# Gated linear attention over 256 tokens: from a chain of sixteen-token chunks to recursive halving in one block

## The chip, the cores and the metric

One NeuronCore of a Trainium2 chip runs the whole kernel. The metric is device time in microseconds, the median of three runs. The profile is one further execution, recorded by the hardware profiler; the time that it took is given beside the span of its trace.

## The reference

One layer of a hybrid decoder over 280 tokens: 256 prompt tokens, 8 decode tokens (one for each of 8 sequences) and 16 meta tokens ahead of the prompt. The layer is a half-step SwiGLU FFN, a mixing stage, and a second half-step FFN, with a norm ahead of each and one at the end. Everything is fp32, D_MODEL is 2048, D_FF is 5632. The mixing stage projects the tokens once and runs two branches side by side: sliding-window attention with 16 heads, and gated linear attention (GLA) with 4 heads of key size 128 and value size 256. Gates then merge the two. The part that the change is about is the GLA branch over the prompt:

```
b   = cumsum(log decay)                        # per token, head and key channel
att[t, s] = sum_d q[t,d] * k[s,d] * exp(b[t,d] - b[s,d])      for s <= t
o   = att @ v + (q * exp(b)) @ S
S   = S * exp(b_last) + (k * exp(b_last - b)).T @ v
```

The difference b[t] - b[s] is never positive for s <= t, but exp(-b[s]) alone can overflow, so the decay can't simply be split into a factor of t and a factor of s over long distances. The meta tokens come first and leave a state S that the prompt starts from; the state after the last prompt token is an output. A decode token updates and reads a state of its own.

## The kernel before

**Slabs.** Each weight matrix is read as slabs of 128 output columns: 16 tiles of 128x128 (11 for the FFN's second matrix). A slab goes through four engines, always with two buffers. SyncE's queue loads it to `raw` (`load_slab`, 1 MB). ScalarE rounds it to `w_hi` (`split_hi`, L623). VectorE writes `w_lo = raw - w_hi` (`split_lo`, L957). TensorE does 48 matmuls of 264 or 280 token columns: hi weights by hi and lo activations (L1352, L1353), then lo weights by hi activations (L1358). Then VectorE takes the sum out of `bank[0]` or `bank[1]` and scales it. `slab_done` counts slabs, `bank_free` their evacuations. A slab waits for the bank of the slab two before it; the split of a slab waits until the slab two before it has been used. There are 404 slabs, in a fixed order: FFN1, `SWA_IN` (12 slabs), `GLA_IN` (16), `GATE_A` (16), `GLA_R` (8), `GATE_B` (12), the merge, `W_OUT`, FFN2. Every engine's program is written out by hand in that order. All that is not a slab is put between two slabs, on each engine by its own code, with semaphores between them.

**The other branch.** During `GLA_IN` the sliding-window attention of the prompt runs between the slabs (`scores`, `turn_scores`, `weigh_values`). During the first eight slabs of `GATE_A` (the loop over `e`) its decode part follows: at e = 3 the scores of eight tokens (L1504, L1505), at e = 7 their values (L1524, L1525), each 32 pairs of fp32 matmuls with 8 columns. Its windows are loaded by ScalarE's DMA queue (`load_windows`), in eleven transfers, eight of them of one row.

**GLA before.** At e = 2 TensorE multiplies the decay's low-rank factor up (L1495); ScalarE and VectorE make log decays of it and `tensor_tensor_scan` sums them into `bc`, in blocks of 32 tokens. After e = 7 the prompt goes through a loop of eight steps (`pair_of_slabs`), each with 32 tokens and two slabs of `GATE_A` or `GLA_R`. In a step, for each of two chunks of 16 tokens, VectorE writes all pairs' differences, 128x1024 (L334, L336); ScalarE takes their exp (L261); VectorE multiplies by keys and queries (L341, L343); and TensorE sums over the channels with 16 fp32 matmuls against a band of ones (`attend`, L386). Between the two chunks a matmul at the boundary does (`attend_across`, L395). Then 12 transposes (`turn`), four products of keys and values for the state (`keys_by_values`, L407), and 16 for the outputs (`outputs`, L423, L425) that lie inside the next step's slab, one after each second k. The step's state update (`new_state`, L359) is on VectorE; GpSimd scales the queries (`queries`, L567) and copies the values (`values`, L563). The last step's outputs and state follow after the loop. The decode part needs the new values split into hi and lo (`v_split`): eight transposes (L1559), ScalarE's zero fill (L868) and two copies (L874), VectorE's two subtractions (L1225). TensorE waits for these (`nv_lo`) ahead of L1585, the first matmul of `GATE_B`.

Of the kernel before, what the change touches and what calls it, by code (L numbers as in the profile page):

```python
# [40 lines left out]
CK = 16  # L41
CP = 2 * CK
NCP = NP_ // CP
# [22 lines left out]
def build_layer(nc, t):  # L66
    ctx = ExitStack()
    with ctx:
# [21 lines left out]
        gadT = sb("gadT", [P, TA])  # L90
# [8 lines left out]
        band = sb("band", [P, 2 * CP - 1])  # L99
# [6 lines left out]
        causal = sb("causal", [CP, 2, GH, CK])  # L106
        a_up = sb("a_up", [P, GH * DK])
# [4 lines left out]
        vbuf = sb("vbuf", [P, 8, CP])  # L112
        eend = sb("eend", [P, GH])


        R = sb("scratch", [P, 6816])
# [21 lines left out]
        sc = at(3060, 2, 4, 272)  # L138
        pT = at(5236, 3, 512)
        v_tok = at(1408, 2, 256)  # L140

        kT_win = at(3232, NS, 2, WIN + 1)
# [7 lines left out]
        v_meta_s = at(3232, NS, 256, parts=NM)  # L150

        oT = at(0, 8, TR)
        spl, mnz = at(5300, GH, TA), at(2112, GH, TA)
        bc = mnz
        scan_keep = at(512, TA)
        S = at(3232, GH, DV)
        Pd = at(4256, CK, GH, CK)
        k_tok = at(5280, 512, parts=CP)
        gv_tok = at(5792, 1024, parts=CP)
        a_smp = a_up[:, TR + GH * CP:TR + GH * CP + GH * NS].rearrange("p (h n) -> p h n", h=GH)  # L160
        kd = a_up[:, TR:TR + GH * CP].rearrange("p (h c) -> p h c", h=GH)

        def halves(tiles):

            return tiles.rearrange("p (x h) c -> p x h c", x=2)


        mid, edl = hT[:, 0:8, M0:TA], hT[:, 8:16, M0:TA]
        qd, attT = proj[:, 16:24, M0:TA], proj[0:CP, 24:32, M0:TA]

# [7 lines left out]
        r_act, r_sg = a_up[:, 0:TR], gadT[:, 0:TR]  # L178
        siga = proj[:, 16:32, 0:TR]
        merged = proj[:, 0:16, 0:TR]  # L180
# [23 lines left out]
        kwin_loaded, kmeta_loaded, vwin_loaded, vmeta_loaded, knew_done, qpad_done = (  # L204
            sem(n) for n in ("kwin_loaded", "kmeta_loaded", "vwin_loaded", "vmeta_loaded", "knew_done", "qpad_done"))
        swa_pe, swa_act, swa_dve, win_out = (sem(n) for n in ("swa_pe", "swa_act", "swa_dve", "win_out"))
        scan_loaded, bias_loaded = sem("scan_loaded"), sem("bias_loaded")
        z_done, prep_act, prep_dve = sem("z_done"), sem("prep_act"), sem("prep_dve")
        (g_eb, g_dl, g_edl, g_kd, g_diff, g_exp, g_pk, g_P, g_att, g_attT, g_kt, g_vt, g_ktok, g_vtok,
         g_vbuf, g_qd, g_o, g_oT, g_kv, g_S) = (sem(n) for n in (  # L210
            "g_eb", "g_dl", "g_edl", "g_kd", "g_diff", "g_exp", "g_pk", "g_P", "g_att", "g_attT", "g_kt",
            "g_vt", "g_ktok", "g_vtok", "g_vbuf", "g_qd", "g_o", "g_oT", "g_kv", "g_S"))
# [9 lines left out]
        g_mid, g_emid, g_kq = sem("g_mid"), sem("g_emid"), sem("g_kq")  # L222
# [15 lines left out]
        def columns(v, width, start=0):  # L238
            return slice(v * width + start, (v + 1) * width) if isinstance(v, int) else bass.ds(v * width + start, width - start)

        def pair_cols(u):
            return slice(M0, TA) if isinstance(u, int) and u == 0 else columns(u - 1, CP)

        def by_half(a):
            return a.rearrange("p h (x c) -> p x h c", x=2)

        def later(u, n=1):
            return not isinstance(u, int) or u > n

        def key_decay(act, u):  # L250
            act.wait_ge(g_dl, u + 1)
            e = edl if later(u, 0) else edl[:, 0:GH]
            act.activation(e, e, ACT.Exp, scale=1.0 / TAU).then_inc(g_edl, 1)

        def mid_decay(act, u):
            act.wait_ge(g_mid, 2 * u)
            act.activation(mid, mid, ACT.Exp, scale=1.0 / TAU).then_inc(g_emid, 1)

        def token_decay(act, c):
            act.wait_ge(g_diff, 2 * c + 2)  # L260
            act.activation(Pd, Pd, ACT.Exp, scale=1.0 / TAU).then_inc(g_exp, 1)  # L261

        def start_decay(act, u):

            act.wait_ge(g_S, 4 * u)
            if later(u):
                act.wait_ge(g_o, u - 1)
            act.activation(eend[:].unsqueeze(2), bc[:, :, columns(u - 1, CP, CP - 1)], ACT.Exp, scale=1.0 / TAU)
            act.activation(halves(qd), by_half(bc[:, :, pair_cols(u)]), ACT.Exp, scale=1.0 / TAU).then_inc(g_eb, 1)

        def to_tokens(act, u):

            n = CP if later(u, 0) else CK
            act.wait_ge(g_vt, u + 1)
            if later(u, 0):
                act.wait_ge(g_kv, u)
            if later(u):
                act.wait_ge(g_o, u - 1)
            act.activation(gv_tok[0:n, 0:512], bank[4][0:n, :], ACT.Copy).then_inc(g_vtok, 1)
            act.activation(gv_tok[0:n, 512:], bank[5][0:n, :], ACT.Copy).then_inc(g_vtok, 1)  # L280
            act.wait_ge(g_kt, u + 1)
            act.activation(k_tok[0:n, :], bank[3][0:n, :], ACT.Copy).then_inc(g_ktok, 1)
# [671 lines left out]
        def _(dve):  # L954
# [141 lines left out]
            for u in range(8):  # L1096
# [4 lines left out]
                if u:  # L1101
                    out_lo(u - 1)
# [622 lines left out]
```

## Time and profile before

| | us |
|---|---|
| median of 3 runs (2499.45 to 2504.62) | 2500.59 |
| profiled execution | 2502.67 |
| its span | 2500.8 |
| TensorE matmuls busy | 2454.7 (98%) |
| TensorE weight loads busy | 2385.5 (95%) |
| VectorE busy | 1369.2 (55%) |
| ScalarE busy | 985.6 (39%) |
| GpSimd busy | 168.4 (7%) |

A fp32 matmul leaves two records in the trace, an fp32r matmul or a transpose one. Matmuls are pipelined, so the duration of one says little; the distance from one start to the next says what it costs. The granted clock is TensorE's, as a share of 2.4 GHz. The stage that the change touches begins at 1071 us in the trace (slab e = 1 of `GATE_A`) and ends at 1391 us (the first matmul of `GATE_B`).

### The profile page before, as it was taken

Reading aid. Unit: us, or ns where it says so; the run is one execution under the profiler, and the core shown is the slowest. Engines: PE = TensorE matmul, PEld = TensorE weight load, DVE = VectorE, ACT = ScalarE, POOL = GpSimd, SP = SyncE. Lnnn points to the kernel's source line nnn. Section 1 sums busy time; section 2 is a strip of 40 time slices with the busy share of each in tenths; the row PEclk is TensorE's granted clock in tenths of the full one; section 3 lists DMA queues with packets and bytes.
Section 4 is the critical chain, followed back from the end, with each engine's and each line's share of the span. In section 5 each row is a group of like instructions: output and inputs, shape, how many; then the busy total and the mean of one; then the engine's idle time right before and its main releaser. Section 6 shows DMA issues by size and latency. Waiting matters only on the chain.

```text
span 2500.8 us, 47207 instructions
## 1 busy us (share of the span) xinstructions
PE 2454.7 (98%) x19106; PEld 2385.5 (95%) x19106; DVE 1369.2 (55%) x1567; ACT 985.6 (39%) x1036; POOL 168.4 (7%) x188
## 2 busy tenths in 40 slices
PE   7999999999999999999999999999999999999997
PEld 6999999999999998898888989999999999999997
DVE  6555554554556545544556465555555555555554
ACT  4333333333333344454545543434333333333332
POOL 2000000000003200000000130021000000000015
PEclk9999999999999999997889999999999999999998
DMA  5445445444544453351112554455555545545544
GB/s 187 173 156 184 168 159 178 170 167 166 186 168 155 167 175 119 118 188 72 67 67 70 191 186 152 169 185 183 176 169 192 181 162 194 184 161 192 184 165 138
DMA packets 67740, 401.72 MB, mean 161 GB/s; under 512 B 8703, under 2 KB 12439, under 8 KB 32199
## 3 DMA queue, kind: packets, MB, share of 16 engines
q1 hardware_dynamic: 62960, 386.86, 44.4%
q0 software_dynamic: 3264, 11.79, 1.3%
q10 hardware_dynamic: 1447, 2.10, 0.3%
q8 instruction: 51, 0.84, 0.1%
q14 instruction: 18, 0.15, 0.0%
HBM read 391.43 MB, written 9.27 MB: 160 GB/s over the span
## 4 chain that ended last, share of the span: by engine, by line
PE 92%; DVE 3%; issue 2%; ACT 1%; POOL 1%; DMA 0%; DVEq 0%; SPq 0%; ACTq 0%; POOLq 0%
PE bank L1352 29%; PE bank L1358 29%; PE bank L1353 28%; PE bank L386 1%; PE bank L407 1%; DVE w_lo L957 1%; PE bank L425 1%; ACT w_hi L623 1%; DVE x_lo L962 1%; PE bank L1466 0%; PE bank L423 0%; PE bank L370 0%; POOL scratch L601 0%; PE bank L1574 0%; PE bank L1464 0%
## 5 line engine op out<-in xcount | busy, mean ns | idle before, releaser
L623 ACT ACTIVATE w_hi<-raw 128x2048 fp32r<-128x2048 f32 (+1 forms) x404 | 705.4, 1746 | 1239.7 <-PE bank L1358 1196.3
L957 DVE TENSOR_TENSOR w_lo<-raw,w_hi 128x2048 fp32r<-128x2048 f32 (+1 forms) x404 | 845.2, 2092 | 469.8 <-ACT w_hi L623 469.6
L1352 PE MATMUL bank<-x_hi,w_hi 128*128 128x264 f32 (+1 forms) x3456 | 906.6, 295 | 16.4 <-DVE x_lo L962 11.5
L1353 PE MATMUL bank<-x_lo,w_hi 128*128 128x264 f32 (+1 forms) x3456 | 888.4, 290 | 0.0
L1352 PEld LDWEIGHTS bank<-x_hi,w_hi 128*128 128x128 f32 x3456 | 658.0, 190 | 40.4 <-issue 19.4
L1353 PEld LDWEIGHTS bank<-x_lo,w_hi 128*128 128x128 f32 x3456 | 658.4, 191 | 0.0
L1352 PE MATMUL bank<-y_hi,w_hi 128*128 128x264 f32 (+1 forms) x2368 | 598.2, 288 | 6.1 <-DVE y_lo L1255 5.6
L1353 PE MATMUL bank<-y_lo,w_hi 128*128 128x264 f32 (+1 forms) x2368 | 596.7, 287 | 0.0
L1358 PE MATMUL bank<-x_hi,w_lo 128*128 128x264 f32 (+1 forms) x3456 | 496.1, 293 | 0.0
L1358 PEld LDWEIGHTS bank<-x_hi,w_lo 128*128 128x128 f32 x3456 | 459.3, 191 | 4.1 <-issue 2.3
L1352 PEld LDWEIGHTS bank<-y_hi,w_hi 128*128 128x128 f32 x2368 | 447.2, 189 | 7.5 <-DVE y_lo L1255 6.9
L1353 PEld LDWEIGHTS bank<-y_lo,w_hi 128*128 128x128 f32 x2368 | 447.9, 189 | 0.0
L1358 PE MATMUL bank<-y_hi,w_lo 128*128 128x264 f32 (+1 forms) x2368 | 322.6, 286 | 0.0
L1358 PEld LDWEIGHTS bank<-y_hi,w_lo 128*128 128x128 f32 x2368 | 303.2, 189 | 0.0
L1011 DVE SCALAR_TENSOR_TENSOR hT<-bank,hT 128x280 f32 (+3 forms) x128 | 56.4, 441 | 116.3 <-PE bank L1358 115.9
L986 DVE TENSOR_TENSOR scratch<-bank,rstd 128x280 f32<-128x280 f32 (+1 forms) x88 | 38.8, 441 | 131.2 <-PE bank L1358 131.2
L503 POOL MEMSET scratch<- 128x280 f32 x4 | 1.3, 334 | 1576.8 <-DVE scratch L986 1457.1
L980 DVE TENSOR_TENSOR scratch<-bank,rstd 128x280 f32<-128x280 f32 (+1 forms) x88 | 38.8, 441 | 119.3 <-PE bank L1358 119.3
L509 POOL TENSOR_TENSOR scratch<-scratch 128x264 f32<-128x264 f32 (+1 forms) x56 | 81.4, 1453 | 4.9
L507 POOL TENSOR_TENSOR scratch<-hT 128x264 f32 (+2 forms) x56 | 37.9, 676 | 125.5 <-DVE hT L1323 68.3
L1048 DVE SCALAR_TENSOR_TENSOR proj<-bank,rstd 128x280 f32<-128x280 f32 (+1 forms) x28 | 12.4, 442 | 58.9 <-PE bank L1358 58.8
L386 PEld LDWEIGHTS bank<-scratch,band 128*32 128x32 f32 x512 | 37.5, 132 | 4.1 <-issue 1.7
(244 smaller groups left out, 1203.4 us busy)
## 6 DMA issues: line engine op xcount, KB each, us to landing
raw<-in_w_in SPq DMA_DIRECT2D x176, 1024.0 KB, 4.8
raw<-in_w_out SPq DMA_DIRECT2D x128, 704.0 KB, 4.0
raw<-in_w_proj SPq DMA_DIRECT2D x52, 1024.0 KB, 4.8
raw<-in_w_merge SPq DMA_DIRECT2D x32, 1024.0 KB, 4.8
raw<-in_w_o SPq DMA_DIRECT2D x16, 1024.0 KB, 4.8
scratch<-in_state_in POOLq DMA_DIRECT2D x8, 512.0 KB, 4.3
out_state_s<-scratch POOLq DMA_DIRECT2D x8, 512.0 KB, 5.3
hT<-in_xT SPq DMA_DIRECT2D x4, 560.0 KB, 7.3
```

The source lines that it names most:

```text
L386: last = pe.matmul(cols, band[:, CP - 1 - m:2 * CP - 1 - m], Pd[:, s], start=(s == 0), stop=(half == 0 and s == CK - 1))
L407: last = pe.matmul(bank[6 + h // 2][:, (h % 2) * DV:(h % 2 + 1) * DV], k_tok[0:n, h * DK:(h + 1) * DK], gv_tok[0:n, h * DV:(h + 1) * DV], ...
L507: pool.tensor_tensor(sq[:, 0:T], h, h, ALU.mult).then_inc(sq_done, 1)
L509: pool.tensor_tensor(acc[:, 0:T], acc[:, 0:T], sq[:, 0:T], ALU.add).then_inc(acc_done, tiles)
L623: act.activation(w_hi[:, b, 0:kt * P], raw[:, b, 0:kt * P], ACT.Copy).then_inc(hi_split, 1)
L957: dve.tensor_tensor(w_lo[:, b, 0:kt * P], raw[:, b, 0:kt * P], w_hi[:, b, 0:kt * P].bitcast(F32), ALU.subtract).then_inc(lo_split, 1)
L980: dve.tensor_tensor(a_n[:, 0:T], bank[0][:, 0:T], rstd[:, 0:T], ALU.mult).then_inc(bank_free, 1)
L986: dve.tensor_tensor(b_n[:, 0:T], bank[1][:, 0:T], rstd[:, 0:T], ALU.mult).then_inc(bank_free, 1)
L1011: dve.scalar_tensor_tensor(hT[:, m, 0:T], bank[b][:, 0:T], 0.5, hT[:, m, 0:T], ALU.mult, ALU.add).then_inc(bank_free, 1)
L1352: pe.matmul(out, w, x[0][:, k, 0:T], start=(k == ks[0]), stop=False)
L1353: pe.matmul(out, w, x[1][:, k, 0:T], start=False, stop=False)
L1358: last = pe.matmul(out, w_lo[:, b, k * P:(k + 1) * P], x[0][:, k, 0:T], start=False, stop=(k == ks[-1]))
```

## The change

The chunks and their loop go. The prompt is taken as two tiles of 128 tokens, and `att` is built by levels: level B (1, 2, 4, ... 64) holds the pairs s, t that lie in the two halves of one block of 2B tokens. For such a pair the decay is exp(b_mid - b_s) times exp(b_t - b_mid), with b_mid at the end of the first half, and both factors are at most 1. So a level is: VectorE takes the differences (`diffs`, two operations of 128x512), ScalarE exp of 128x1024 (`decays`), VectorE the products with keys and queries (`products`, two of 128x512), TensorE eight fp32 matmuls 128x128 by 128 columns (`level`: 4 heads, 2 tiles), VectorE puts the pairs of the level into `att` by a mask (`place`, two `copy_predicated` of 128x512, PSUM source, uint8 mask). The diagonal is a level of its own (`D_`), level 64 has 64 columns, level 128 only four matmuls; ScalarE places these two. There are no passes by GpSimd in the levels; it makes the six masks during FFN1.

The levels are spread over 24 slabs, one or so behind each. The meta state is made at e = 8 and 9, the values turned at e = 10 and 11, the end-decayed keys turned at e = 14, the final state at e = 15 (eight matmuls of 256 columns), the outputs at e = 16 to 23 (three matmuls each of 256, 256 and 128 columns). The gates' sigmoids move from the slab that makes them to e >= 16, two each. The log decays move ahead to `SWA_IN`. The last rows of the value windows are loaded by SyncE's queue, which waits for `so_done`, `kv_out` and `knew_done` ahead of it and of the slab behind, and the new rows by GpSimd's. The first state of the decode part is loaded once the prompt's state has been written out. Tiles move: `oT` to `proj`, `merged` in two halves, the states' slots in another order.

```diff
-            def pair_of_slabs(half, v, more=True):
-                ...
-                slab(half, 0, KD, x, TR, beside=outputs_beside if later(v, 0) else None)
-                attend(pe, 2 * v, 0)
-                slab(half, 1, KD, x, TR, beside=state_beside if later(v, 0) else None)
-                attend(pe, 2 * v + 1, 1)
-                attend_across(pe, v + 1)
-                if more:
-                    turn(pe, v + 2)
...
+        def level(pe, lev):
+            if lev > D_:
+                pe.wait_ge(kq_mul, MULS[lev])
+            a, b = (k_T, q_T) if lev == D_ else (kq[KQ_OF[lev]],) * 2
+            for tt in range(2):
+                for h in range(GH):
+                    s_cols = slice(tt * P, tt * P + P)
+                    ...
+                        last = pe.matmul(bank[BANKS[lev][tt]][:, h * P:h * P + P], a[:, h, s_cols], b[:, h, s_cols], start=True, stop=True)
+            last.then_inc(lev_pe, 1)
...
+        def place(dve, lev):
+            dve.wait_ge(lev_pe, lev + 1)
+            for tt in range(2):
+                src = bank[BANKS[lev][tt]][:].rearrange("p (h t) -> p h t", h=GH)
+                dst = att[tt][:, :, 0:P]
+                ...
+                    dve.copy_predicated(dst, cast(masks[:, lev - L1].unsqueeze(1), dst), src).then_inc(att_done, 1)
...
@@ block.sync
+            load_slab(t["w_proj"][16:17, 0], GATE_A + 2, 0, KD)
+            sp.wait_ge(so_done, 8)
+            sp.wait_ge(kv_out, 32)
+            sp.wait_ge(knew_done, 1)
+            sp.dma_start(v_win[VROWS:WIN - 1], t["v_cache"][VROWS:WIN - 1]).then_inc(vlast_loaded, 16)
+            load_slab(t["w_proj"][16:17, 1], GATE_A + 2, 1, KD)
...
@@ block.vector, the loop over e (24 slabs)
+                if e == 9:
+                    place(dve, L8)
+                    diffs(dve, L32)
+                    products(dve, L16)
+                if e == 10:
+                    place(dve, L16)
+                    diffs(dve, L64)
+                    products(dve, L32)
...
@@ block.tensor
             slab(SWA_IN, 1, KD, x, TR)
+            pe.wait_ge(gadT_done, 1)
+            for h in range(GH):
+                last = pe.matmul(bank[2 + h][:, 0:TA], a_up[:, h * DK:(h + 1) * DK], gadT, start=True, stop=True)
...
+                if e == 15:
+                    pe.wait_ge(kt_done, 2)
+                    ...                      # 8 matmuls of 256 columns: the state
+                    pe.wait_ge(att_done, ATTS[L128])
+                    ...                      # 8 transposes: nv_tr
+                if e >= 16:
+                    j, h = e - 16, (e - 16) // 2
+                    ...
+                    if j >= 2:
+                        pe.wait_ge(o_out, j - 1)
+                    pe.matmul(out[:, 0:NP_], S_meta[:, h, (j % 2) * P:(j % 2 + 1) * P], kq[0][:, h, :], start=True, stop=False)
+                    pe.matmul(out[:, 0:NP_], v_tok[:, 0, cols], att[0][:, h, :], start=False, stop=False)
+                    pe.matmul(out[:, P:NP_], v_tok[:, 1, cols], att[1][:, h, :], start=False, stop=True).then_inc(o_pe, 1)
```

ScalarE at e >= 16: `split_hi`, the sigmoid for r, two gates' sigmoids, the copy to `y3_hi` (after VectorE's product), the copy of the output tile to `oT`. The code after the loop (zero fill, copies and subtractions of `v_split`) is as before; on TensorE nothing but `nv_lo`'s wait stands between the outputs of e = 23 and L1585.

## Rows read from the trace of the kernel before

**Rows 1.** The page, busy time by engine, and the clock in 40 slices.
```profile
PE 2454.7 (98%) x19106; PEld 2385.5 (95%) x19106; DVE 1369.2 (55%) x1567; ACT 985.6 (39%) x1036; POOL 168.4 (7%) x188
...
PEclk9999999999999999997889999999999999999998
```
**Rows 2.** The page, chain of work that ended last, share of the span by engine.
```profile
PE 92%; DVE 3%; issue 2%; ACT 1%; POOL 1%; DMA 0%; DVEq 0%; SPq 0%; ACTq 0%; POOLq 0%
```
**Rows 3.** Busy time in three stretches: start:end, length, engines, granted clock, DMA share.
```profile
927.00:1070.00 143.00, 140.90 (x1000) 123.44 (x1001) 81.06 (x157) 62.10 (x129) 0.00 (x0) 0.99 0.33 117
1103.50:1111.00 7.50, 7.50 (x51) 7.37 (x50) 0.00 (x0) 1.25 (x4) 0.51 (x1) 0.79 0.67 266
1160.60:1378.60 218.00, 216.94 (x1622) 187.37 (x1621) 127.72 (x181) 112.63 (x142) 6.30 (x13) 0.88 0.20 73
```
**Rows 4.** Timeline of TensorE: start us, duration us, then line and shapes.
```profile
1071.03 0.37 PE L1352 MATMUL bank<-x_hi,w_hi 128*128 128x264 f32 x1
...
1077.07 0.64 PE L1464 MATMUL bank<-scratch 16*64 16x512 f32 x1
...
1079.93 0.39 PE L1352 MATMUL bank<-x_hi,w_hi 128*128 128x264 f32 x1
...
1085.97 2.15 PE L1495 MATMUL bank<-gadT,a_up 16*128 16x280 f32 x8
...
1088.05 0.39 PE L1352 MATMUL bank<-x_hi,w_hi 128*128 128x264 f32 x1
...
1094.01 0.28 PE L1504 MATMUL bank<-scratch 128*128 128x8 f32 x2
...
1103.55 0.59 PE L1352 MATMUL bank<-x_hi,w_hi 128*128 128x264 f32 x1
...
1132.30 0.29 PE L1524 MATMUL bank<-scratch,proj 128*128 128x8 f32 x2
...
1145.59 1.89 PE L370 MATMUL bank<-ident,vbuf 128*32 128x128 f32 x8
...
1151.97 0.59 PE L1352 MATMUL bank<-x_hi,w_hi 128*128 128x264 f32 x1
...
1160.61 0.80 PE L386 MATMUL bank<-scratch,band 128*32 128x64 f32 x11
...
1391.18 1.22 PE L1585 MATMUL bank<-small_r 40*128 40x512 f32 x2
```
**Rows 5.** Timeline of TensorE, fp32 matmuls (x2 is one matmul) and transposes.
```profile
1070.24 1.04 PE L1456 MATMUL bank<-ident,scratch 128*128 128x128 f32 x8
...
1137.74 0.59 PE L1525 MATMUL bank<-scratch 16*128 16x8 f32 x2
1138.27 0.59 PE L1524 MATMUL bank<-scratch,proj 128*128 128x8 f32 x2
...
1382.12 0.40 PE L425 MATMUL bank<-proj,scratch 32*128 32x32 f32 x2
1382.45 0.41 PE L423 MATMUL bank<-proj,scratch 128*128 128x32 f32 x2
...
1467.10 0.60 PE L1599 MATMUL bank<-proj,ones 128*128 128x264 f32 x2
1467.55 0.61 PE L1600 MATMUL bank<-proj,ones 128*128 128x264 f32 x2
```
**Rows 6.** Groups by line over the span: count, busy us, mean ns of one.
```profile
L957 DVE TENSOR_TENSOR w_lo<-raw,w_hi 128x2048 fp32r<-128x2048 f32 (+1 forms) x404 | 845.2, 2092 | 469.8 <-ACT w_hi L623 469.6
L623 ACT ACTIVATE w_hi<-raw 128x2048 fp32r<-128x2048 f32 (+1 forms) x404 | 705.4, 1746 | 1239.7 <-PE bank L1358 1196.3 <-DMA raw<-in_w_out 32.6 <-DMA raw<-in_w_in 6.8
L341 DVE TENSOR_TENSOR scratch<-scratch,proj 128x1024 f32<-128x1024 f32 x16 | 19.5, 1216 | 0.0
```
**Rows 7.** Timelines of ScalarE and VectorE ahead of `GATE_B`.
```profile
1386.03 1.04 ACT L868 ACTIVATE small_r<-ones 40x1024 fp32r<-40x1024 f32 x1
...
1388.35 1.28 DVE L1225 TENSOR_TENSOR small_r<-bank,small_r 8x512 fp32r<-8x512 f32 x2 [1.77 <-ACT small_r L874]
```

More of the change, by code:

```diff
@@ L1465, in weigh_values @@
                 for kc in range(u % 2 + 1):
[L1466 removed]
+                    last = pe.matmul(out, v_rows[:, kc, cols], pT[:, kc], start=False, stop=(kc == u % 2))
                 last.then_inc(so_done, 1)
@@ L1490, in _ @@
                 if e == 2:
-                    pe.wait_ge(solo_done, 16)
                     pe.wait_ge(pT_done, 24)
-                    pe.wait_ge(gadT_done, 1)
-                    for h in range(GH):
-                        last = pe.matmul(bank[4 + h][:, 0:TA], a_up[0:RANK, h * DK:(h + 1) * DK], gadT[0:RANK], start=True, stop=True)
-                    last.then_inc(z_done, 1)
+                    level(pe, D_)
                 if e == 3:
@@ new lines, in _ @@
+                if e == 9:
+                    pe.wait_ge(meta_tok, 3)
+                    pe.wait_ge(swa_dve, 12)
+                    for h in range(GH):
+                        last = pe.matmul(bank[2 + h // 2][:, (h % 2) * DV:(h % 2 + 1) * DV], k_meta[:, h * DK:(h + 1) * DK],
+                                         gv_meta[:, h * DV:(h + 1) * DV], start=True, stop=True)
+                    last.then_inc(smeta_pe, 1)
+                    pe.wait_ge(att_done, ATTS[L4])
+                    level(pe, L8)
@@ new lines, in _ @@
+                if e in (10, 11):
+                    if e == 10:
+                        level(pe, L16)
+                        pe.wait_ge(smeta_done, 2)
+                    else:
+                        pe.wait_ge(att_done, ATTS[L8])
+                        level(pe, L32)
+                        pe.wait_ge(vt_done, 2)
+                    for j in range(8):
+                        last = pe.transpose(bank[2 + j // 4][:, (j % 4) * P:(j % 4 + 1) * P],
+                                            proj[:, GV + j, (e - 10) * P:(e - 9) * P], ident[:])
+                    last.then_inc(vt_pe, 1)
@@ new lines, in _ @@
+                if e == 12:
+                    pe.wait_ge(att_done, ATTS[L16])
+                    level(pe, L64)
+                if e == 13:
+                    pe.wait_ge(att_done, ATTS[L32])
+                    level(pe, L128)
+                if e == 14:
+                    pe.wait_ge(kq_mul, MULS[END])
+                    pe.wait_ge(vt_done, 4)
+                    for tt in range(2):
+                        for h in range(GH):
+                            last = pe.transpose(bank[2 + tt][:, h * P:h * P + P], kq[1][:, h, tt * P:tt * P + P], ident[:])
+                    last.then_inc(kt_pe, 1)
```

803 lines of the change are left out of this document (393 added, 410 removed).

## The prediction

> **What bounds the kernel now.** I read the page's busy times first, then its chain, then the stretches of the stage that changes, then single starts there. TensorE's matmuls are busy 98% of the span, its weight loads 95%; VectorE 55%, ScalarE 39%, GpSimd 7% [rows 1]. The chain that ended last is 92% TensorE and 3% VectorE [rows 2]. So time goes only with what TensorE has to do, with its clock, and with waits that stop it. The clock is full in nearly all slices and falls in the middle, where this stage lies [rows 1]. There the eight steps of the chunk loop take 218.0 us at a mean clock of 0.88, with TensorE busy for 216.9 of it, VectorE for 127.7, ScalarE for 112.6, GpSimd for 6.3 [rows 3]. It is TensorE's own work, not a wait.
>
> A slab between two pieces of other work takes 1077.07 - 1071.03 = 6.04 us [rows 4]. The loop holds 16 slabs, 96.6 us; the other 121.4 us are the chunks' small matmuls, transposes, and slabs and fillers run at the lower clock. That is the stock that the change can draw on.
>
> **The sum.** I compare the stretch from the start of slab e = 1 to the first matmul of `GATE_B`: before, 1391.18 - 1071.03 = 320.2 us [rows 4]. After, TensorE does in it:
>
> 1. The same 23 slabs: 23 x 6.04 = 138.9.
> 2. Kept work: the values of the last window unit 1079.93 - 1077.07 = 2.9, the decode scores 1103.55 - 1094.01 = 9.5, the decode values 1145.59 - 1132.30 = 13.3 [rows 4], four transposes at 0.1, 0.4: together 26.1.
> 3. The clock is low behind both decode pieces, which stay: slab e = 4, with its transposes, took 7.5 at a clock of 0.79 [rows 3], 1.3 over; the slab at 1151.97 took 8.6, 2.6 over [rows 4]: 3.9.
> 4. The levels: 68 fp32 matmuls with 128 stationary columns (8 in each of eight levels, the diagonal among them, and 4 in level 128). The trace has none with 128 moving columns. With 32 columns one costs 1382.45 - 1382.12 = 0.33; with 264, 1467.55 - 1467.10 = 0.45 [rows 5]. These are the ends. At 264 columns the stream sets the pace, and 128 columns of it would be 0.22, less than the 0.33 that a matmul costs whose stream is short; so a floor from the weights holds at 128 columns too, and I take 0.335. The levels 1 and 4 come right behind the decode pieces, at the low clock, where a matmul of 8 columns costs 1138.27 - 1137.74 = 0.53 [rows 5]: 16 x 0.53 = 8.5. The other 52 x 0.335 = 17.4. Together 25.9 (upper end 52 x 0.45 + 8.5 = 31.9).
> 5. Meta state, values, keys, final state, new values: 12 + 16 + 8 + 8 = 44 transposes at 1071.03 - 1070.24 over 8 = 0.1 [rows 4, 5], 4.4; 12 matmuls of 256 columns at 0.445, 5.3; 9.7 in all, 10.5 with the changes between kinds of matmul that the eight gaps show (about 0.1 each).
> 6. Outputs: 8 x (0.445 + 0.445 + 0.335) = 9.8.
> 7. A new wait at the end. ScalarE and VectorE make `v_split` only after their bodies of e = 23. Before, from the start of the zero fill to the end of the subtractions took 1388.35 + 1.28 - 1386.03 = 3.6 [rows 7], with outputs and state products of TensorE over it. After, TensorE has nothing left but 1.2 of outputs. Counted from the end of slab 23: split of the hi weights 1.9, VectorE's lo 2.1 [rows 6] (means of 1.7 and 2.1, and the handover), its product for r 0.4, ScalarE's copy of it 0.4 and of the output tile 0.4, then the 3.6: TensorE may go on 9.0 after the slab, and is free at 1.4. Stall 7.5. Its low clock afterwards replaces one that is there already: before, the loop's last work also ended at a low clock.
>
> Sum: 138.9 + 26.1 + 3.9 + 25.9 + 10.5 + 9.8 + 7.5 = 222.6, against 320.2: 97.6 less. The decay's matmuls (1088.05 - 1085.97 = 2.1 [rows 4]) only move to `SWA_IN`, so 2.1 comes back there: 95.5 less. The profiled execution took 2502.67, which makes 2407.2; it stood 2.1 above the median of 2500.59, which would make 2405.1. I say 2406.
>
> **What is hidden, and by what.** Most of the change is passes of VectorE and ScalarE. Between fillers TensorE now takes 7.3 to 10 us for a slab. In the fullest bodies (e = 9, 10, 11) VectorE has: evacuation 0.4, wait for hi until 1.9, lo until 4.1, then `place`, `diffs`, `products`, six passes of 128x512. A pass of 128x1024 is 1.22 [rows 6], so 512 elements are above 0.61, taken as 0.68: 4.1 in six. Done at 8.2 after the slab; the next slab ends at e = 9 after 6.04 + 1.8 + 2.7 = 10.5, at e = 10 and 11 after 9.7. Nothing waits: TensorE needs products one slab later and a level's place before the next use of its banks, two fillers later. `copy_predicated` is not in the trace. The lower bound is the 0.61 of half a pass; the upper that of four cycles' worth of the same, 2.1, which is the row of 2048 elements; then the body is 11.0 long and three bodies push TensorE by 1 us each. ScalarE has 1.9 and an exp of about 1.1 that starts when the differences are there, at about 7 us: its next split starts up to 1.5 us late, and slab e+2 needs it 4 us later. At e = 3 the queue behind ScalarE's exp of level 2 (it comes 16 us after the slab, since level 1 sits behind the decode scores) is the split of slab 6, due at 21 us. SyncE's queue now waits for `so_done`, which rises 2.9 us after slab 1 and so about when that slab's lo split frees the buffer anyway; what is behind it, the load of slab 5, is due 20 us later, and with 2 MB of windows beside it at the rate of a slab per 5 us it is there by about 16. Cost 0; if the cover is gone, a few us once. In `SWA_IN` the added passes of ScalarE at n = 3 (two of 128x1120 and up to two table loads) come to about 7 us beside a slab of 5.9: one split is late by 1, with 4 of slack. GpSimd gives up 6.3 us in 218 [rows 3] and nothing that TensorE waited for at length; its masks are made in FFN1, where it idles.
>
> **Rivals.**
> (a) The clock falls around the levels too. The loop before ran at 0.88 [rows 3], with single fp32 matmuls strewn into the slabs. A level is different in that it is compact, 2.7 us of 128-column matmuls, and the stage of the prompt's window scores, which has such fillers between its slabs, held 0.99 over 143 us [rows 3]. If it falls nevertheless, each of nine fillers costs 1.5 more and its next slab 2.6: 37 us, 2443. The Trainium skill (TensorE: Matmul & The Clock Gate, Part 4: PE-mode transpose) says that transposes don't keep the clock up as matmuls do. By this rule the four bodies with 8 or more transposes would drop it, 4 x 2.6 = 10 us, 2416; the trace disagrees, as the twelve transposes ahead of slab 1 stood in a slab that still took 6.04.
> (b) Weight loads aren't hidden by the stream: then a 128-column matmul costs 0.33 + 0.22 = 0.55, and 52 + 8 of them 13 more: 2419. Against it: 264 columns would then cost over 0.7, and the row says 0.45.
> (c) A hand-over that I have as hidden is late in several bodies (the predicated copy at its upper bound, or ScalarE's split behind a late exp): 24 bodies, 0.5 to 1 us each: 2418 to 2430.
> (d) The stall at the end is hidden or shorter than I have it, and the levels go at the pace of their columns alone: 0.12 x 52 + 4 = 10 us less: 2396.
> (e) Slower than before: VectorE becomes the bound of the stage through `copy_predicated`. Twelve of them would have to cost the 95 us and the slack of about 2 us in each of six bodies: 9 us for one, thirteen times the price that I take and four times that of a pass with 2048 elements. It decides from there on: at 10 us each, 2515.
> (f) The change does not take the work from TensorE that it says: only if the levels need several times the matmuls that I count; the count is in the diff.
>
> **How the numbers follow.** The sum as it stands 0.72 (own range 2398 to 2414), (a) 0.08, (b) 0.03, (c) 0.10, (d) 0.04, (e) 0.02, (f) 0.01. The range reaches down to (d) and over most of (c) and the upper end of term 4: 2396 to 2430. Two runs of this kernel are told apart from about 0.2%, 5 us. Faster 0.97, same 0.01, slower 0.02.
>
> **What would show it.** In the profile after: 222.6 us from slab e = 1 to the first matmul of `GATE_B`; starts 0.33 apart within a level; the mean clock near 1 between e = 9 and 23; an idle time of about 7 us ahead of L1585's counterpart, released by VectorE; VectorE busy about 8 us in each of the bodies 9 to 11, and no wait of TensorE for `kq_mul` or `att_done`. I would be wrong if the clock is below 0.95 there, if level matmuls stand 0.45 or more apart, or if TensorE waits for a hi or lo split between e = 3 and e = 16.

## The result, and the profile after

| | before | after |
|---|---|---|
| median us (lowest to highest) | 2500.02 (2496.6 to 2504.62, 4 runs) | 2394.74 (2394.1 to 2395.75, 4 runs) |
| ratio, 95% interval | | 0.9578 [0.9562, 0.9595] |
| profiled execution, its span | 2502.67, 2500.8 | 2395.09, 2393.1 |
| mean granted clock | 0.976 | 0.986 |

The changed kernel is 4.2% faster, 105.3 us. The forecast was 2406 with a range of 2396 to 2430: the direction and the mechanism are as forecast, the gain is 11 us larger, and the time lies 1.3 us below the range.

The page after, the lines that answer to those of [rows 1, 2]: busy time by engine, the clock in 40 slices, the chain by engine.

```profile
PE 2341.6 (98%) x18338; PEld 2304.8 (96%) x18338; DVE 1313.1 (55%) x1476; ACT 912.9 (38%) x948; POOL 177.4 (7%) x209
...
PEclk9999999999999999999899999999999999999998
...
PE 94%; DVE 3%; ACT 1%; issue 1%; POOL 1%; DMA 0%; DVEq 0%; SPq 0%; ACTq 0%; POOLq 0%
```

TensorE is as full as before. Its busy time fell by 113 us, a little more than the span did (107.7). VectorE and ScalarE lost work too; that this bought nothing by itself is shown for VectorE's differences alone (e4). The dip of the clock in the middle has shrunk from three slices below 9 to one.

The stretches after, with start:end, length, busy time of TensorE, its weight loads, VectorE, ScalarE and GpSimd (instructions in brackets), granted clock, DMA share and GB/s. The first is the prediction's own (slab e = 1 to the first matmul of `GATE_B`, 320.2 before [rows 4]), the second the decode scores with level 1, the third levels 8 to 128 with all their slabs (its counterpart in [rows 3] is the loop at 0.88), the fourth the outputs.

```profile
1075.65:1284.09 208.44, 200.20 (x1498) 193.36 (x1496) 109.03 (x132) 86.07 (x115) 8.63 (x15) 0.94 0.44 153
1098.16:1110.97 12.81, 12.81 (x83) 12.04 (x81) 2.73 (x2) 2.33 (x3) 1.38 (x2) 0.60 0.87 337
1168.00:1230.00 62.00, 62.00 (x495) 60.56 (x494) 39.53 (x45) 28.17 (x28) 1.12 (x2) 1.00 0.40 145
1234.00:1283.00 49.00, 42.21 (x328) 41.36 (x326) 24.33 (x28) 28.04 (x47) 1.07 (x2) 0.99 0.48 176
```

208.4 us where 222.6 were forecast. The clock is 1.00 over five levels and their transposes, and TensorE has no gap there.

TensorE's timeline after: start us, duration us, line and shapes. L1319 begins a slab, L314 is a level of eight fp32 matmuls (x16 in the trace, since each leaves two records), L1471 and L1496 begin the decode's scores and values, L312 is level 64, L1562 to L1564 are the outputs of one slab, L1587 is the first matmul of `GATE_B`.

```profile
1075.65 0.37 PE L1319 MATMUL bank<-x_hi,w_hi 128*128 128x264 f32 x1
...
1090.51 1.95 PE L314 MATMUL bank<-proj 128*128 128x128 f32 x16
1092.21 0.37 PE L1319 MATMUL bank<-x_hi,w_hi 128*128 128x264 f32 x1
...
1098.16 0.28 PE L1471 MATMUL bank<-scratch 128*128 128x8 f32 x2
...
1107.60 3.61 PE L314 MATMUL bank<-scratch 128*128 128x128 f32 x16
1110.97 0.37 PE L1319 MATMUL bank<-x_hi,w_hi 128*128 128x264 f32 x1
...
1116.91 0.27 PE L1478 MATMUL bank<-ident,scratch 128*128 128x128 f32 x1
...
1137.57 0.28 PE L1496 MATMUL bank<-scratch,proj 128*128 128x8 f32 x2
...
1151.51 3.78 PE L314 MATMUL bank<-scratch 128*128 128x128 f32 x16
1154.94 0.52 PE L1319 MATMUL bank<-x_hi,w_hi 128*128 128x264 f32 x1
...
1160.99 0.60 PE L1505 MATMUL bank<-ident,proj 128*16 128x128 f32 x4
...
1194.97 1.89 PE L312 MATMUL bank<-scratch 128*128 128x64 f32 x16
1196.67 0.37 PE L1319 MATMUL bank<-x_hi,w_hi 128*128 128x264 f32 x1
...
1226.72 0.59 PE L1563 MATMUL bank<-scratch 128*128 128x256 f32 x2
1227.15 0.38 PE L1564 MATMUL bank<-scratch 128*128 128x128 f32 x2
1227.29 0.37 PE L1319 MATMUL bank<-x_hi,w_hi 128*128 128x264 f32 x1
...
1275.82 0.38 PE L1564 MATMUL bank<-scratch 128*128 128x128 f32 x2
1284.09 1.22 PE L1587 MATMUL bank<-small_r 40*128 40x512 f32 x2 [7.88 <-DVE small_r L1186]
```

Three readings. A level takes 1092.21 - 1090.51 = 1.70 us, 0.21 for each of its eight matmuls, not 0.335. Level 64, with half the columns, takes 1196.67 - 1194.97 = 1.70 us as well. The slabs behind the two pieces of the decode take 1116.91 - 1110.97 = 5.94 and 1160.99 - 1154.94 = 6.05 us, where 7.5 and 8.6 were seen before and forecast again. And TensorE idles 7.88 us ahead of `GATE_B`, released by VectorE, as forecast (7.5).

VectorE's timeline in the body behind the slab that ends at 1177.92 (start us, us, line, and in brackets the idle time before it):

```profile
1178.12 0.43 DVE L1074 TENSOR_TENSOR proj<-bank,rstd 128x264 f32<-128x264 f32 x1 [0.37 <-PE bank L1325]
1180.12 2.29 DVE L879 TENSOR_TENSOR w_lo<-raw,w_hi 128x2048 fp32r<-128x2048 f32 x1 [1.57 <-ACT w_hi L538]
1182.33 1.35 DVE L327 COPY_PREDICATED scratch<-masks,bank 128x512 f32<-128x512 uint8 x2
1183.57 0.67 DVE L260 TENSOR_TENSOR scratch<-bcum 128x512 f32<-128x512 f32 x1
1184.16 1.28 DVE L297 TENSOR_TENSOR scratch<-scratch,proj 128x512 f32<-128x512 f32 x2
```

It is done at 1185.44, 7.5 us after the slab, inside a distance of 8.5 from slab to slab. The predicated copies take 0.73 each over the run, differences and products 0.68.

### The profile page after: what moved, and what is told of

Its sections match the earlier page's. It is cut to its first block, busy times and chain, and to the rows that moved or that the text cites. A ratio compares the mean times of both kernels' runs of the same rounds, so it can differ in the third digit from the quotient of the medians.

```text
span 2393.1 us, 45066 instructions
## 1 busy us (share of the span) xinstructions
PE 2341.6 (98%) x18338; PEld 2304.8 (96%) x18338; DVE 1313.1 (55%) x1476; ACT 912.9 (38%) x948; POOL 177.4 (7%) x209
## 4 chain that ended last, share of the span: by engine, by line
PE 94%; DVE 3%; ACT 1%; issue 1%; POOL 1%; DMA 0%; DVEq 0%; SPq 0%; ACTq 0%; POOLq 0%
PE bank L1319 30%; PE bank L1320 30%; PE bank L1325 29%; DVE w_lo L879 1%; ACT w_hi L538 1%; PE bank L314 1%; DVE x_lo L884 1%; PE bank L1437 0%; POOL scratch L516 0%; PE bank L1576 0%; PE bank L1435 0%; PE bank L1497 0%; PE bank L1471 0%; DVE scratch L1227 0%; PE bank L1496 0%
## 5 line engine op out<-in xcount | busy, mean ns | idle before, releaser
L1319 PE MATMUL bank<-x_hi,w_hi 128*128 128x264 f32 (+1 forms) x3456 | 895.0, 293 | 16.2 <-DVE x_lo L884 11.5
L1319 PEld LDWEIGHTS bank<-x_hi,w_hi 128*128 128x128 f32 x3456 | 656.5, 190 | 30.5 <-issue 10.7
L1319 PE MATMUL bank<-y_hi,w_hi 128*128 128x264 f32 (+1 forms) x2368 | 597.9, 287 | 6.1 <-DVE y_lo L1215 5.7
L1325 PE MATMUL bank<-x_hi,w_lo 128*128 128x264 f32 (+1 forms) x3456 | 471.6, 288 | 0.0
L1319 PEld LDWEIGHTS bank<-y_hi,w_hi 128*128 128x128 f32 x2368 | 447.0, 189 | 7.5 <-DVE y_lo L1215 6.9
L1325 PEld LDWEIGHTS bank<-x_hi,w_lo 128*128 128x128 f32 x3456 | 448.7, 189 | 0.0
L911 DVE TENSOR_TENSOR scratch<-scratch 128x280 f32<-128x280 f32 (+1 forms) x88 | 38.9, 442 | 3.1
```

Of the source, the lines that this page charges most:

```text
L911: dve.tensor_tensor(s32[:, 0:T], act_a[:, 0:T], b_n[:, 0:T], ALU.mult).then_inc(s_done, 1)
L1319: pe.matmul(out, w, x[0][:, k, 0:T], start=(k == ks[0]), stop=False)
L1325: last = pe.matmul(out, w_lo[:, b, k * P:(k + 1) * P], x[0][:, k, 0:T], start=False, stop=(k == ks[-1]))
```

## The experiments

All were timed against the kernel before, whose median in these runs was 2499.9 to 2502.4. Differences below are taken to the changed kernel's 2394.74. It was not timed again beside them, so a difference of under 3 us counts only where a trace shows it too.

### e2_twice: what does a level cost?

```
-            for tt in range(2):
+            for tt in [0, 1] * 2:
```

> The changed kernel, with every level's matmuls done twice on TensorE into the same banks (68 fp32 matmuls with 128 stationary columns more, nothing else). Theory: such a matmul costs what its columns stream, 0.21 us behind one of its own shape (the diagonal's eight took 1.7 in the trace), so 68 x 0.21 = 14.5 us more, 2409. Rival (my prediction's term): 0.335 each, a floor of the weight loads: 22.8 more, 2417.5. Either way nothing else should move, since VectorE's and ScalarE's bodies get longer covers.

Measured: 2410.09 (2408.15 to 2410.48), 15.3 us more; ratio to before 0.9638 [0.9622, 0.9654]. 68 more matmuls in 15.35 us are 0.23 each. In its trace the diagonal's level takes 3.49 us, so the eight added matmuls cost 0.22 each. So 0.21 to 0.22 is what a level's matmul costs the kernel, not just a spacing in one place. At 0.335 it would have been 22.8.

### e5_cols32: is there a floor under short matmuls?

```
-  last = pe.matmul(bank[..][:, h*P:h*P+P], a[:, h, s_cols], b[:, h, s_cols], ...)
+  for c in range(0, P, 32):          # levels 8, 16, 32
+      last = pe.matmul(bank[..][:, h*P+c:h*P+c+32], a[:, h, s_cols],
+                       b[:, h, tt*P+c:tt*P+c+32], ...)
```

> The matmuls of levels 8, 16 and 32 (24 of 128 columns) are cut into 96 of 32 columns, each group of four with the same stationary tile; the result is the same. It asks what the old bands paid for. Theory A (a matmul of few columns has a price of its own, in which columns hardly count; the old form had 32-column bands at 0.33 us): 96 x 0.33 - 24 x 0.21 = 26.6 us slower than the changed kernel, 2421. Rival B (the columns set the price; 128 columns take 0.21, so 32 take 0.055): no change, 2395. Rival C (a loading of the stationary tile is what is paid, some 0.1 us each): 96 x 0.11 - 5.0 = 5.5 us slower, 2400.

Measured: 2424.93 (2424.52 to 2426.61), 30.2 us more; ratio 0.9698 [0.9682, 0.9715]. The size is near theory A's, but its mechanism is not what the trace shows. TensorE in level 8 of this kernel; first the timeline, then windows (start:end, length, TensorE's busy time and records, granted clock, DMA share, GB/s):

```profile
1167.32 1.99 PE L1516 MATMUL bank<-scratch 16*128 16x256 f32 x8
1169.24 11.35 PE L316 MATMUL bank<-scratch 128*128 128x32 f32 x64
1180.40 0.57 PE L1322 MATMUL bank<-x_hi,w_hi 128*128 128x264 f32 x1
```

```profile
1169.30:1171.30 2.00, 2.00 (x20) 1.00 0.00 0
1174.00:1178.00 4.00, 4.00 (x20) 0.50 0.73 262
1180.40:1188.70 8.30, 8.30 (x49) 0.68 0.01 2
```

A window also counts the records that reach over its ends, so the pace is better read from single starts. While the clock is full, the first 24 records of L316 start 0.11 us apart: a matmul of 32 columns, two records, takes 0.22. So do the matmuls of 128 and of 64 columns inside the levels of the changed kernel (1090.62 to 1090.84 within the diagonal, 1195.03 to 1195.25 within level 64). Behind those 24 records the granted clock falls to 0.50, the lower of the two levels, and a matmul takes 0.43, again as one of 128 columns does in level 1 (eight in 3.37 us); the slab behind runs at 0.68 and takes 8.30 instead of 5.95.

So there is a floor, but at 0.22 us and not at 0.33, and 128 columns lie at it: shorter matmuls are dear by their number, and a second time through the clock. In all three groups the weight loads start 0.11 us apart, two to a matmul, whatever the columns. That fits a floor made by the loads. At 128 columns half of the 0.43 that 256 columns take would give the same 0.22, so whether loads or columns set the pace there is not separated.

### e6_rows32 and e11_rows_grouped: where did 0.33 come from?

The prediction's 0.33 was the distance between a matmul with 128 rows and one with 32 [rows 5]. e6 makes the levels alternate in this way, by leaving out 96 of the 128 channels of heads 1 and 3; e11 does the same matmuls, those of 128 rows first.

```
+ rows = slice(0, P if h % 2 == 0 else 32)
- last = pe.matmul(..., a[:, h, s_cols], b[:, h, s_cols], ...)
+ last = pe.matmul(..., a[rows, h, s_cols], b[rows, h, s_cols], ...)
  # e11 as well:
- for tt in range(2):
-     for h in range(GH):
+ for h in (0, 2, 1, 3):
+     for tt in range(2):
```

> Leaves out 96 of the 128 channels of heads 1 and 3 in every level of 128 columns, so that the stationary tiles alternate between 128 and 32 partitions; as many matmuls and columns as before. It asks whether the pace of 0.33 us per matmul, which the prediction took from rows in which stationary tiles of different shapes alternate, comes from the alternation. Theory A (it does): 56 matmuls from 0.21 to 0.33 us, 6 to 7 us slower than the changed kernel, 2401. Rival B (the pace goes by columns alone): no change, 2394.7. Rival C (a tile of 32 rows loads sooner): up to 2 us faster.

> As the kernel of e6_rows32 (leaves out 96 of the 128 channels of heads 1 and 3 in the levels of 128 columns), but each level does its four matmuls of 128 rows first and then its four of 32 rows: the stationary tile's rows change once or twice in a group of eight, not eight times. In e6_rows32 such a group of eight took 3.22 us at full clock, 0.40 each, where eight of one shape take 1.70. Theory A (each change of rows costs the load of the stationary tile, 0.19 us, that is otherwise hidden): the group takes 1.7 + 0.2 to 0.4 us, the clock stays at 1.00, and the kernel comes within 4 us of the changed one, 2395 to 2399. Rival B (tiles of 32 rows are slow by themselves, or lower the clock by themselves): as e6_rows32, 2418.

Measured: e6 2418.22 (2417.27 to 2419.0), 23.5 more; ratio 0.9669 [0.9653, 0.9685]. e11 2403.7 (2400.33 to 2408.05), 9.0 more; ratio 0.961 [0.9592, 0.9629]. The diagonal's level and the slab behind it; e6's timeline:

```profile
1090.94 3.29 PE L315 MATMUL bank<-proj 128*128 128x128 f32 x16
1094.16 0.39 PE L1320 MATMUL bank<-x_hi,w_hi 128*128 128x264 f32 x1
```

e11's:

```profile
1091.31 2.13 PE L315 MATMUL bank<-proj 128*128 128x128 f32 x16
1093.38 0.39 PE L1320 MATMUL bank<-x_hi,w_hi 128*128 128x264 f32 x1
```

Windows of e6, that level and the slab behind it:

```profile
1090.94:1094.16 3.22, 3.22 (x19) 1.00 1.06 266
1094.16:1101.64 7.48, 7.48 (x50) 0.77 1.06 334
```

At full clock eight matmuls take 1.70 us with one shape, 3.22 alternating and 2.07 sorted. Theory A holds for the cause, and the price of a change of rows is 1.52 / 8 = 0.19 us; the sorted group, with one change inside and one to the slab behind it, gives (2.07 - 1.70) / 2 = 0.19 too. For 32 columns it was less: 0.33 in [rows 5] against 0.22 in e5.

The weight loads (PEld) show where it comes from. The first change of rows in e6:

```profile
1091.05 0.57 PE L315 MATMUL bank<-proj 128*128 128x128 f32 x2
1091.25 0.18 PEld L315 LDWEIGHTS bank<-proj 32*128 32x128 f32 x1
```

The load of the 32-row tile starts 0.20 us after the last record of the matmul ahead of it. In the changed kernel, where all tiles have one shape, the next load starts together with that record (both at 1090.62). So at a change of rows the load is not run ahead. The Trainium skill (TensorE: Matmul & The Clock Gate, Part 3: Packing small matmuls, The mechanism) says that a load overlaps running matmuls only when its row group differs; the same section also lets a load into a background weight buffer run ahead. 128 rows behind 128 rows overlap here, which the second would allow and the first would not. That the change between 32 and 128 rows does not overlap is said by neither.

The totals are larger than theory A expected, 6 to 7 for e6. At 0.19 the 56 matmuls of the seven levels of 128 columns come to 10.6 at full clock. In e6's trace these levels are 13.8 us longer, as three run at a lower clock, and the slabs behind five of them take 7.3 to 8.2, together 8.7 more. In e11 three slabs still ran low (7.16 and 8.27 behind the decode's pieces and their levels, 8.37 behind level 8), which its theory A did not expect either. Whether the clock goes with the tiles of 32 rows or with the changes that are left is open.

### e3_first: does a level bring the clock back?

```
  # level(pe, L1) from behind the decode scores to ahead of them,
  # level(pe, L4) from behind the decode values to ahead of them
```

> The changed kernel, with the matmuls of level 1 and of level 4 ahead of the decode scores and the decode values on TensorE instead of behind them. In the changed kernel's trace the slabs behind these two levels take 5.94 and 6.05 us, where before, with no level between, they took 7.5 and 8.6. Theory: the level's dense matmuls right behind the decode piece bring the clock back before the slab begins, at their own cost (3.3 and 4.1 us for the two in place of 1.7 each). Then with the levels ahead the slabs take 7.3 to 8.6 again, the levels 1.7: 4 us more in the slabs, 4 us less in the levels, together within 1 us of 2394.7. Rival: the slabs are fast for another reason (the decode piece leaves the clock up in this kernel): then the slabs stay at 6 and the kernel is 4 us faster, 2391.

Measured: 2393.88 (2393.77 to 2396.8), 0.9 less, no difference; ratio 0.958 [0.9564, 0.9596]. Windows of the two slabs that now stand right behind a piece of the decode:

```profile
1107.46:1115.84 8.38, 8.38 (x51) 0.68 0.06 20
1151.37:1159.92 8.55, 8.55 (x49) 0.66 0.00 0
```

They are 2.4 and 2.5 us longer than the 5.94 and 6.05 that they take behind a level, 4.9 together. The two levels take 1.79 and 1.78 in place of 3.37 and 3.43, 3.2 less, and the two pieces of the decode themselves, 8.76 and 13.10 in place of 9.44 and 13.94, another 1.5 less. (The expectation's 4.1 us for level 4 came from the old length of the decode's values, 13.29.) So the level pays most of the time of low clock in the slab's place. It is a shift, not a gain.

### e8_before_batch: was it the strewing of small matmuls through the slabs?

The kernel before, with each chunk's outputs in one piece behind the slab.

```
- slab(half, 0, KD, x, TR, beside=outputs_beside if later(v, 0) else None)
+ slab(half, 0, KD, x, TR)
+ if later(v, 0):
+     for n in range(16):
+         outputs(pe, v, n)
```

> The kernel BEFORE, with the 16 output matmuls of each step of the chunk loop behind its first slab in one piece instead of strewn into the slab (seven steps; nothing left out). Theory: a good part of the 121 us that the loop took beyond its slabs was not the number of small matmuls but their mixing: a slab with outputs in it took 15.4 us where the slab alone takes 6.04 and 16 matmuls in one piece 16 x 0.335 = 5.4. So 4 us less in each of seven steps, 28 us, and some more by the clock: 2465 to 2472. Rival: only the count matters, or what is gained is lost in the wait for the output tile's copy that now follows at once (0.5 to 1 us a step): within 5 us of 2500.

Measured: 2507.1 (2502.27 to 2510.87, 10 runs), 0.25% slower than the kernel before; ratio 1.0025 [1.0016, 1.0035]. The theory fell. TensorE's timeline in one of its pieces (x2 is one matmul):

```profile
1181.93 0.41 PE L423 MATMUL bank<-proj,scratch 128*128 128x32 f32 x2
1182.27 0.63 PE L425 MATMUL bank<-proj,scratch 32*128 32x32 f32 x2
1182.83 0.64 PE L423 MATMUL bank<-proj,scratch 128*128 128x32 f32 x2
```

In the piece these matmuls of 32 columns with changing rows cost 0.34 at full clock and 0.56 from where it has fallen. A slab and its outputs take 13.3 to 13.4 us in the first three such steps, where the kernel before took 14.6, 13.7 and 15.4, so something is gained. But the clock is lower behind the piece: the step's second slab, with the state's products in it, takes 10.2 to 10.3 in place of 9.3, and a whole first step is 1.0 us longer (30.52 against 29.56). Bringing the small matmuls together is worth nothing here as long as their number and form stay.

### e7_place4 and e4_pool: how much room has VectorE?

```
  # e7: the copy under the mask, four times
+ for i in range(3):
+     dve.copy_predicated(dst, cast(masks[:, lev - L1].unsqueeze(1), dst), src).then_inc(again, 1)
+     dve.wait_ge(again, 3 * (2 * (lev - L1) + tt) + i + 1)
  # e4: every diffs(dve, lev) becomes, on GpSimd,
+ pool.wait_ge(lev_pe, free + 1)
+ diffs(pool, lev)
```

> Every copy under the mask is done four times, one behind the other (68 copies instead of 17, at 0.68 us each): VectorE's body of a level grows by 4.1 us, from 8.0 to 12.1 us, against 8.51 us from slab to slab. It measures how much room VectorE has. Theory A (VectorE has only what its idle rows show, 1.6 to 2.5 us a body, and every slab waits for its low part): six bodies give 1.6 to 2.5 us each and the two beside the decode pieces nothing: 8 to 20 us slower than the changed kernel, 2403 to 2415. Rival B (the copies lie in a buffered part, and the levels are not on the path): within 2 us of the changed kernel. Rival C (the level's products come late and add to it): 30 us or more slower.

> The differences of all ten levels go back to GpSimd, beside the new form of the levels; nothing else moves. Theory A (VectorE is not the bound: its body of one slab and one level is 8.0 to 8.5 us long, with 0.4 to 1.6 us idle in it, against 8.51 us from slab to slab): the same time as the changed kernel, 2394.7 within 1.5 us, and the levels stay 1.70 us each between two slabs of 5.95. Rival B (GpSimd's passes, 1.06 to 1.45 us each on 128x512 where VectorE takes 0.68, or their effect on VectorE's passes, come late): each level's products are late by 1 us or more and TensorE waits in front of each level: 5 to 15 us slower than the changed kernel, 2400 to 2410.

Measured: e7 2417.97 (2417.03 to 2418.32), 23.2 more; ratio 0.9668 [0.9652, 0.9684]. The expectation miscounted: there are 12 copies, now 48, at a mean of 0.74, so 4.4 us more in each of six bodies, and its upper end of 20 us was passed. TensorE's waits in the levels of this kernel (line, what it waited for, us in total, times, longest):

```profile
PE bank L315 <- DVE scratch L298: 7.3, 3, 3.3
PE bank L313 <- DVE scratch L298: 3.6, 1, 3.6
PE bank L1489 <- DVE scratch L1141: 3.2, 1, 3.2
PE bank L1517 <- DVE y_lo L1154: 1.6, 1, 1.6
```

In the changed kernel this view has one line, 0.4 us for L297. Here 15.7 us are waits. The other 7.5 us of the 23.2 are slabs and levels at a lower clock (theory A, with the clock's price on top): the slab behind the wait of 3.2 takes 7.45. 36 more copies are 26.5 us, of which 15.7 came through as waits, so VectorE's room was at most (26.5 - 15.7) / 6 = 1.8 us a body. It was less if the slower stretches of TensorE gave VectorE part of that cover: by the whole loss it is (26.5 - 23.2) / 6 = 0.5. e4: 2394.6 (2394.04 to 2395.62), the same as the changed kernel; ratio 0.9575 [0.9559, 0.9591]. A difference takes GpSimd 1.1 to 1.3 us (3.1 once) and VectorE 0.68, and neither is waited for. Which engine takes the differences, a named part of the change, is worth nothing.

### e1_hoist and e9_hoist_pick: the idle time ahead of GATE_B

```
  # e1, ScalarE, in the body of e = 14 and 15 instead of behind the loop:
+ if e == 14: act.activation(v_split..., scale=0.0).then_inc(nv_zero, 1)
+ if e == 15: (wait nv_tr, nv_zero; the two copies to v_split)
  # e1, VectorE: the subtractions behind the final state's pass, not behind the loop
  # e9 as well, ScalarE:
+ if e == 15: ...; pick_token(0)
```

> The changed kernel, with the zero fill, the two copies and the two subtractions of the new values' split moved from behind the loop into the bodies of e = 14 and 15. In the changed kernel's trace TensorE idles 7.9 us ahead of the first matmul of GATE_B, released by the second subtraction, and the slab behind it starts at the low clock and takes 7.45 us where others take 5.95. Theory: the idle time and that slab's low clock both go, 7.9 + 1.5 = 9.4 us less than the changed kernel, 2385.5. Rival: another wait is just behind it (the decode state's load, which waits for the last output, or VectorE's state update): then the idle time turns up under another name in the next slabs and the time falls by less than 4 us. Second rival: the low clock after the wait is not of the wait's making and stays: 7.9 less.

> As the kernel of e1_hoist (v_split filled during the loop over slabs), and ScalarE also makes the first column of pick there, in place of behind its whole loop. Theory A (TensorE's 7.9 us in front of GATE_B was a chain of waits on ScalarE and VectorE behind their loops, and pick was the last link): the idle time goes, and with it the low clock of the slab behind it (7.45 for 5.95 us): 7.9 + 1.5 = 9.4 us faster than the changed kernel, 2385.3. Rival B (a third link is just behind, the first new products of VectorE or the bank of the matmul): some 2 to 4 us more than e1_hoist gave, 2388 to 2390. Rival C (the time is given back at the next wait inside GATE_B, whose slabs wait for the states' loads): 2392 as e1_hoist.

Measured: e1 2392.33 (2390.78 to 2392.83), 2.4 less; ratio 0.9568 [0.9552, 0.9583]. e9 2386.11 (2383.39 to 2386.71), 8.6 less; ratio 0.954 [0.9527, 0.9553]. TensorE's row in e1:

```profile
1281.70 1.19 PE L1588 MATMUL bank<-small_r 40*128 40x512 f32 x2 [4.75 <-ACT small_r L796]
```

and in e9:

```profile
1274.10 0.73 PE L1588 MATMUL bank<-small_r 40*128 40x512 f32 x2
1274.75 0.39 PE L1320 MATMUL bank<-x_hi,w_hi 128*128 128x264 f32 x1
...
1281.12 0.70 PE L1588 MATMUL bank<-small_r 40*128 40x512 f32 x2 [0.24 <-DVE scratch L1195]
```

With `v_split` early, the next operand of the same matmul was late, `pick`, also left behind ScalarE's loop, and 4.75 of the 7.88 us stayed. With both early the first matmul waits for nothing and the second `L1588` for 0.24 us, and the slab between runs in 6.37 instead of 7.45 us. Of the expected 9.4 us, 8.6 came.

### e10_late_masks and e12_both: 2.8 us in FFN1, and the best version

```
+ pool.wait_ge(bank_free, 40)
  for i in range(6):
      make_mask(i)
```

> GpSimd makes the six masks after some twenty slabs of FFN1 and not at 21 to 36 us. The changed kernel is 2.8 us later than the kernel before when the levels' stretch begins; its granted clock was low at 34 to 46 us, the only place before the attention where it differs. Theory A (the masks, by their traffic or by lengthening VectorE's passes around the sum of squares, leave TensorE without work where the clock is then lowered): the clock stays at 1.00 there and the kernel is 2.8 us faster, 2391.9. Rival B (the dip is a matter of the phase in which TensorE's wait for the sum of squares falls, which is in both kernels): no change, 2394.7. Rival C (the masks disturb wherever they stand): no change in the time, the dip moves.

> e9_hoist_pick and e10_late_masks together, as a version to beat both kernels. If the two are independent, their gains add: 2394.7 less 9.4 less 2.8 = 2382.5; if the clock's dip at 34 to 46 us is a matter of phase (rival B of e10_late_masks), 2385.3, as e9_hoist_pick.

TensorE at 38 to 42 us (window, length, busy time and records, granted clock, DMA share, GB/s), in the kernel after:

```profile
38.00:42.00 4.00, 4.00 (x19) 0.50 0.12 51
```

in e12_both, masks late:

```profile
38.00:42.00 4.00, 4.00 (x25) 0.72 0.10 43
```

in e5_cols32, masks early:

```profile
38.00:42.00 4.00, 4.00 (x33) 1.00 0.13 51
```

Measured: e10 2395.31 (2393.41 to 2396.29), no change; ratio 0.9577 [0.9564, 0.9591]. e12 2383.84 (2383.47 to 2385.66), 10.9 less; ratio 0.9533 [0.952, 0.9546]. The dip is absent with early masks (e5) and there with late ones (e12), so the masks are not its cause. It is absent in e10 without a gain in the median. In e10's profile the slab that starts at 64.13 us in the changed kernel starts 2.75 us earlier, but slab e = 1 only 1.3: between 920 and 940 us the granted clock is 0.83 in place of 0.91. The dip was in 10 of the 12 profiles of kernels of the new form and in neither of two of the old (before, e8). What sets it is open. e12's 2383.84 lies between its two expected times. It has the lowest median, 4.7% under the kernel before; its range and e9's overlap, so the late masks are not shown to add anything.

## Why the prediction was right in its mechanism and wrong in its size

By its terms, each read from starts in the trace after. The decode's pieces are 1107.60 - 1098.16 = 9.44 and 1151.51 - 1137.57 = 13.94, the levels behind them 3.37 and 3.43:

| term | forecast | measured |
|---|---|---|
| 1 and 3, 23 slabs and their low clock | 142.8 | 137.7 |
| 2, kept work | 26.1 | 26.7 |
| 4, levels | 25.9 | 18.1 |
| 5, transposes and 12 matmuls | 10.5 | 9.8 |
| 6, outputs | 9.8 | 8.0 |
| 7, wait ahead of `GATE_B` | 7.5 | 8.1 |
| sum | 222.6 | 208.4 |
| decay matmuls in `SWA_IN` | +2.1 | +1.7 |
| FFN1 | 0 | +2.8 |

2407.2 - 14.2 - 0.4 + 2.8 = 2395.4, against the profiled 2395.09.

**The step that failed is term 4's pace**: "so a floor from the weights holds at 128 columns too, and I take 0.335". There is a floor, and 128 columns lie at it, but it is 0.22 us and not 0.335: 128 columns (the levels), 64 (level 64) and 32 (e5) all take 0.22 within a group of one shape, and e2 confirms it as a price. The 0.335 came from a row that alternates 128x128 with 32x128 stationary tiles [rows 5], and e6 and e11 show that the change of rows costs extra, 0.19 at 128 columns. The prediction's own 0.22 from the 264-column row was the right number, set aside for a floor that was mis-sized. The 52 matmuls at full clock took 11.3 us and not 17.4, the 16 at the low clock 6.8 and not 8.5: 7.8 us of the 14.2. In the outputs the third matmul stands only 0.14 ahead of the next slab (1227.29 - 1227.15), not 0.335: most of term 6's 1.8.

**Term 3 missed where the clock comes back.** The level behind each decode piece takes most of the low clock in the slab's place (e3), and the forecast counted it twice: 0.53 a matmul in the level (0.42 measured) and 1.3 and 2.6 in the slab. Terms 1 and 3 together are 5.1 too high, of which 2 is a slab of 5.95 instead of 6.04 and 3.1 this double count. The 8.6 itself was read behind 6.4 us of the old chunks' transposes and state products [rows 4], not right behind the decode; e3's 8.55 right behind it says that the number held.

**Right:** TensorE's own work was the bound and the loop at 0.88 the stock. The clock stayed at 1.00 through levels 8 to 128, against rival (a) with its sentence on transposes: eight of them stand in each of four fillers of the 62 us at 1.00, and twelve in a fifth that it did not count, at e = 8, whose next slab takes 6.04 us. The loads were hidden between tiles of one shape, against (b). No hand-over was late but for 0.36 us once, against (c), with a room of 0.5 to 1.8 us a body by e7. The predicated copy took 0.73 where 0.68 was taken, against (e). The wait of 7.5 came, with its releaser. Rival (d) was half right: its number for the pace was the real one, its shorter stall was not. That its 2396 lies so near the measured time is luck: the pace gave 6 of its 10 us as it says, but the other 4 did not come from the stall. The range ended at (d), with no room below it for terms 3 and 6 erring the same way.

**Not seen:** that `pick` was a second late operand of the matmul (it costs nothing while `v_split` is later), and the clock's dip in FFN1.

## What to carry to other kernels

A price for a small matmul must come from a row with the same sequence of stationary shapes: the change between 32 and 128 rows alone was 0.19 us, nearly as much as the matmul. With 128x128 stationary tiles an fp32 matmul of fewer than 128 columns was no cheaper here, so halving the columns (level 64) saved nothing. Eight matmuls of 128 columns between two slabs left the clock at 1.00, and 32 matmuls of 32 columns took it to 0.50 and the next slab to 8.30: count what a form of work does to the clock of the next slab too, and count it once. When an operand is moved off a path, list every operand of the waiting instruction: the second one here held 60% of the wait.

## What was not expected of the hardware

- Fp32 matmuls with 128x128 stationary tiles, one behind the other: 0.22 us at full clock for 128, 64 and 32 columns alike, 0.43 for 128 and 32 columns at the lower level.
- At a change between 128 and 32 rows the weight load starts 0.20 us after the record that it starts together with where the shape stays the same, and the matmul costs 0.19 more.
- Eight matmuls of 128 columns at 0.40 each because of changing rows, TensorE shown as busy for all 3.22 us at a clock of 1.00, and the slab behind them at 0.77 (7.48 us).
- A level of eight matmuls behind a piece of the decode (the two together at a clock of 0.60) was enough for the slab behind it to run at 1.00 in 5.94 us.
